# Splitting the keys four tiles ahead, with two more of ten heads copied by ScalarE

## The reference

```
p = h @ w_in[l]
q_a, k_a, v_a, q_b, k_b, v_b = split(p)        # 8 + 2 + 2, then 8 + 8 + 8 heads of 64
q_a = _axial_rope(_rms_norm(q_a, qn_a[l]), row_pos, col_pos)   # likewise k_a; q_b, k_b normed only
o_a = _window_gqa_latent(q_a, k_a, v_a, k_ac, v_ac, sink_a[l])
o_b = _neighbourhood_latent(q_b, k_b, v_b, k_bc, v_bc, rpb_b[l])
```

## Time and profile before

| | |
|---|---|
| three runs | 2680.24, 2682.34 (median), 2683.26 us |
| the profiled execution: its own time | 2682.12 us |
| its span, first to last instruction | 2680.3 us |
| mean granted TensorE clock | 0.960 of full |
| PE busy | 2469.3 us, 92% |
| DVE, ACT, POOL busy | 1621.1, 1061.1, 359.8 us |
| last input panel ends, keys begin | about 362.6 us |
| first scores of the attention | 395.06 us |
| barrier behind the attention | about 757.6 us |

### The profile page before, as it was taken

The page is one execution under the profiler, slowest core; times in us unless marked ns, Lnnn a source line. Parts: engine busy times, 40 slices in busy tenths (PEclk is TensorE's granted clock), DMA queues, the critical chain, the costliest instruction groups (busy, mean ns, idle before and its releaser), DMA issues. The chain is left out here.

```text
span 2680.3 us, 42340 instructions
## 1 busy us (share of the span) xinstructions
PE 2469.3 (92%) x15597; PEld 2129.4 (79%) x15597; DVE 1621.1 (60%) x2701; ACT 1061.1 (40%) x2101; POOL 359.8 (13%) x507
## 2 busy tenths in 40 slices
PE   4799979988969799999999989997897999999998
PEld 2689877777859688888888889995795888878886
DVE  3523237776764977777677942007529777756677
ACT  1422235555641433333344432124435544444443
POOL 2566312221110200000000010003203000000001
PEclk8899989999979899999999999997898999999999
DMA  8233320000032132333275431110131444377463
GB/s 288 94 111 118 117 52 3 1 1 1 1 125 80 71 103 91 118 102 102 99 271 177 154 123 32 48 32 13 47 127 63 157 146 157 130 253 254 133 187 116
DMA packets 189033, 288.15 MB, mean 108 GB/s; under 512 B 11704, under 2 KB 109948, under 8 KB 188540
## 3 DMA queue, kind: packets, MB, share of 16 engines
q1 hardware_dynamic: 188860, 285.84, 31.9%
HBM read 219.46 MB, written 67.34 MB: 107 GB/s over the span
## 5 line engine op out<-in xcount | busy, mean ns | idle before, releaser
L378 PE MATMUL ps<-w_hi,ht_hi 128*128 128x256 f32 x1744 | 504.3, 289 | 18.5 <-DVE w_lo L363 9.8
L379 PE MATMUL ps<-w_lo,ht_hi 128*128 128x256 f32 x1744 | 498.5, 286 | 0.0
L380 PE MATMUL ps<-w_hi,ht_lo 128*128 128x256 f32 x1744 | 498.4, 286 | 0.0
L378 PEld LDWEIGHTS ps<-w_hi,ht_hi 128*128 128x128 f32 x1744 | 338.6, 194 | 35.4 <-DVE w_lo L363 11.7
L379 PEld LDWEIGHTS ps<-w_lo,ht_hi 128*128 128x128 f32 x1744 | 338.6, 194 | 0.0
L380 PEld LDWEIGHTS ps<-w_hi,ht_lo 128*128 128x128 f32 x1744 | 338.2, 194 | 0.0
L363 DVE TENSOR_TENSOR w_lo<-stage,w_hi 128x2048 fp32r<-128x2048 f32 x31 | 73.7, 2377 | 220.9 <-ACT w_hi L359 220.9
L1696 PE MATMUL ps<-ff_b_hi,ff_a_hi 128*128 128x512 f32 x448 | 174.5, 390 | 2.6 <-DVE ff_b_lo L1684 1.4
L1698 PE MATMUL ps<-ff_b_hi,ff_a_lo 128*128 128x512 f32 x448 | 174.3, 389 | 0.0
L1697 PE MATMUL ps<-ff_b_lo,ff_a_hi 128*128 128x512 f32 x448 | 174.3, 389 | 0.0
L1454 PE MATMUL ps<-ht_hi,swiglu_w_hi 128*128 128x512 f32 x352 | 138.2, 393 | 10.1 <-DVE tmp L1964 7.7
(11 more groups left out here) (361 smaller groups left out, 5748.4 us busy)
## 6 DMA issues: line engine op xcount, KB each, us to landing
ff_a_raw<-ff_act_dram SPq DMA_DIRECT2D x112, 256.0 KB, 2.8
stage<-w_in SPq DMA_DIRECT2D x23, 1024.0 KB, 5.2
swiglu_a_raw<-swiglu_act_dram SPq DMA_DIRECT2D x77, 256.0 KB, 3.0
stage<-w_mod SPq DMA_DIRECT2D x16, 1024.0 KB, 5.5
ff_stage<-w_ff SPq DMA_DIRECT2D x16, 1024.0 KB, 5.4
ff_act_dram<-ff_act_sums SPq DMA_DIRECT2D x16, 1024.0 KB, 4.3
ff_act_dram<-ff_acts SPq DMA_DIRECT2D x16, 768.0 KB, 5.7
swiglu_stage<-w_up SPq DMA_DIRECT2D x11, 1024.0 KB, 5.2
```

What stands on the lines that cost most here:

```text
L378: pe.matmul(bank, a, wh[:, k, :], start=(k == 0), stop=False)
L379: pe.matmul(bank, a, wl[:, k, :], start=False, stop=False)
L380: mm = pe.matmul(bank, b, wh[:, k, :], start=False, stop=(k == KT - 1))
```

## The change

`k_split` becomes four buffers of their own, at offsets 0, 5120, 10240 and 24576 of the ring. Those lie on `stage`, on slot 0 of w_hi and on slot 0 of w_lo, which the ninth panel does not use. ScalarE's `hi` of tiles 0 to 3 moves into the ninth panel, behind its copies of rows 4 to 7; `hi` and `lo` of tile j + 4 then follow the copies out of tile j. ScalarE copies heads 8 and 9 too, so that it has six heads of ten, and VectorE four. The loops are written out. The first `hi` waits for the last weight split, the end of the eighth panel, and the normed and rotated keys.

```diff
-    k_split = at("k_split", [2, 10, P], F32, ring)
+    k_split = [at(f"k_split{i}", [10, P], F32, ring + x) for i, x in enumerate((0, 5120, 10240, 24576))]
@@ keys_pe
+            pe.wait_ge(dense_evac, D_O)
+            for j in range(10):
                 pe.wait_ge(ks_lo, j + 1)
-                if late:
+                if j >= 2:
                     pe.wait_ge(kt_a, j - 1)
                     pe.wait_ge(kt_v, j - 1)
                 for h in range(10):
-                    mm = pe.transpose(ps[:, 3 * b + h // 4, (h % 4) * P:(h % 4 + 1) * P], k_split[:, b, h, :], ident[:, :])
+                    mm = pe.transpose(ps[:, 3 * (j % 2) + h // 4, (h % 4) * P:(h % 4 + 1) * P], k_split[j % 4][:, h, :], ident[:, :])
                 mm.then_inc(kt_tr, 1)
+        def key_hi(act, j):
+            if j == 0:
+                act.wait_ge(w_lo_done, P_O)
+                act.wait_ge(*panel_used(P_O - 2))
+                act.wait_ge(hg_done, 10)
+                act.wait_ge(roped, ROPED)
+            if j >= 4:
+                act.wait_ge(kt_tr, j - 3)
+            act.activation(k_split[j % 4][:, :, 0:HD].bitcast(F32R),
+                           row_tile(k_nat, j, 0, KVW).rearrange("p (h d) -> p h d", d=HD), ACT.Copy).then_inc(ks_hi, 1)
@@ keys_act
+            for j in range(10):
                 act.wait_ge(kt_tr, j + 1)
+                act.activation(kt[:, 0:4, j * P:(j + 1) * P], ps[:, 3 * (j % 2), :].rearrange("p (h n) -> p h n", n=P), ACT.Copy)
+                act.activation(kt[:, 8:10, j * P:(j + 1) * P], ps[:, 3 * (j % 2) + 2, 0:2 * P].rearrange("p (h n) -> p h n", n=P),
+                               ACT.Copy).then_inc(kt_a, 1)
+                if j + 4 < 10:
+                    key_hi(act, j + 4)
@@ keys_dve
+            for j in range(4):
+                lo(j)
+            for j in range(10):
+                dve.wait_ge(kt_tr, j + 1)
+                dve.tensor_copy(kt[:, 4:8, j * P:(j + 1) * P], ps[:, 3 * (j % 2) + 1, :].rearrange("p (h n) -> p h n", n=P)).then_inc(kt_v, 1)
+                if j + 4 < 10:
+                    lo(j + 4)
@@ ScalarE's program
+            for n, panel in enumerate(X_PANELS[:8]):
+                heads_act(act, panel, P_X + n + 1, NT, 0, D_X + NT * n, 6 + NT * n)
+            for j in range(NT):
+                act.wait_ge(dense_done, D_X + NT * 8 + j + 1)
+                act.activation(v_nat[:, j, X_PANELS[8][1]:X_PANELS[8][1] + PN], ps[:, j % 4, 0:PN], ACT.Copy).then_inc(dense_evac, 1)
+                if j >= 4:
+                    key_hi(act, j - 4)
             keys_act(act)
```

More of the change, by code:

```diff
@@ L544, in keys_pe @@
         def keys_pe(pe):
-            def tile(j, b, late):
+            pe.wait_ge(dense_evac, D_O)
+            for j in range(10):
                 pe.wait_ge(ks_lo, j + 1)
-                if late:
+                if j >= 2:
                     pe.wait_ge(kt_a, j - 1)
                     pe.wait_ge(kt_v, j - 1)
-                else:
-                    pe.wait_ge(dense_evac, D_O)
                 for h in range(10):
-                    mm = pe.transpose(ps[:, 3 * b + h // 4, (h % 4) * P:(h % 4 + 1) * P], k_split[:, b, h, :], ident[:, :])
+                    mm = pe.transpose(ps[:, 3 * (j % 2) + h // 4, (h % 4) * P:(h % 4 + 1) * P], k_split[j % 4][:, h, :], ident[:, :])
@@ L554, in tile @@
                 mm.then_inc(kt_tr, 1)
[L555 to L559, removed]
-        def keys_act(act):
[L563 to L571, removed]
-                act.wait_ge(kt_tr, j + 1)
[L573 to L586, removed]
@@ L588, in keys_dve, with lo @@
         def keys_dve(dve):
-            def lo(j, b):
+            def lo(j):
                 dve.wait_ge(ks_hi, j + 1)
[L591 to L597, removed]
+                dve.tensor_tensor(k_split[j % 4][:, :, HD:P], row_tile(k_nat, j, 0, KVW).rearrange("p (h d) -> p h d", d=HD),
+                                  k_split[j % 4][:, :, 0:HD], ALU.subtract).then_inc(ks_lo, 1)
@@ L1163, in _ @@
             act_c(act)
-            for n, panel in enumerate(X_PANELS):
-                heads_act(act, panel, P_X + n + 1 if n < 8 else None, NT, 0, D_X + NT * n, 6 + NT * n)
+            for n, panel in enumerate(X_PANELS[:8]):
[5 more added lines that the diff above has]
+                    key_hi(act, j - 4)
             keys_act(act)
```

## The result

The changed kernel took 2660.4 us in the median of five runs (2658.33 to 2666.94), the kernel before 2682.34 us in five beside it (2680.03 to 2684.53). Two more sets of five runs of the same changed kernel (experiments 1 and 12) had medians of 2658.51 and 2664.0 us, with ratios of 0.9922 (0.9908 to 0.9936) and 0.9938 (0.9924 to 0.9951). Over all fifteen the mean is 2662.4 and the median 2663.7 us, from 2656.95 to 2667.08. Over the 52 runs of the kernel before that were made in this study the mean is 2680.5 and the median 2680.3 us, from 2675.17 to 2685.51. So the change is worth some 18 us by the means and 16.6 by the medians.

The account below looks back on a forecast made before the run. The keys were taken as a chain of waits with no engine full. Attention starting 15.5 us earlier, less 0.3 for POOL, gives 15.2 off 2682.12: 2666.9, put at 2667.0 for the median; range 2663.5 to 2674.

Parts of the forecast that it names:

- The start: First key tile: its transposes wait only for the panel's last copy and start at 363.1, not 364.68.
- The steady state: Inside the keys, per tile: TensorE 1.09, ScalarE 1.41, VectorE 1.39 us, none alone the bound; pace 1.55.
- the ring: Keys: waits through ScalarE's copies and `hi`, VectorE's `lo` and copy, and TensorE take 4.64 us for three tiles.
- POOL's contention: POOL's first two query splits fall beside `lo` of tiles 3 and 4 and the first copies: 0.3 us lost.
- The clock: TensorE runs the keys at full speed, busy 75%; a 3.4 us low stretch, if one comes, costs 1 us.
- The loops: Key loops: writing them out costs nothing, as in the dense panel's written-out rows.
- The sum, and behind the keys: Keys save 15.5 - 0.3 = 15.2 us; later stages pass it on, low stretches there up to 1 us each.
- The range: Whole kernel: 2663.5 (sum, 2 us of low stretches, 1.5 of runs' spread) to 2674 (low clock throughout).
- The low clock in the changed keys: Rival, chance 0.14: half speed through the keys, 2.15 us a tile, 8.3 us saved, 2674 us.
- the slower ring: Rival, chance 0.10: five hand-overs in the keys take 0.2 us more each; 9 to 12 saved, 2670 to 2673.
- no change: Rival, chance 0.04: something else holds the attention's start at about 395; time within 0.2% (5.4 us).
- slower: Rival, chance 0.04: low clock reaches into the attention; 82 us of it needed to be slower by 0.2%.

Follow-up runs that it names:

- experiment 12: Changed kernel a third time, with no edit: 2664.0 us, ratio 0.9938.
- experiment 5: Changed kernel with the four first `hi` splits put behind the last panel instead of inside it: 2663.74 us, ratio 0.9947.
- experiment 6: Changed kernel with two buffers, first two tiles split early, the others two tiles ahead, tile by tile: 2665.47 us, ratio 0.9954.
- experiment 7: Changed kernel with three buffers, three tiles split early and the others three tiles ahead: 2662.15 us, ratio 0.9935.
- experiment 9: Kernel before with key loops written out and 10 or 16 unused constant transposes in each TensorE wait of the keys: 2670.01 us, ratio 0.9961.
- experiment 2: Kernel before with only the three key loops written out: 2679.59 us, ratio 0.9998.
- experiment 10: Kernel before with three chained useless ScalarE copies, some 3.2 us, as first work behind the attention's barrier: 2684.82 us, ratio 1.0019.
- 4: Changed kernel with 15 chained useless ScalarE copies, some 17 us, between the last key copy and the attention: 2683.17 us, ratio 1.0009.
- 8: Changed kernel with three short ScalarE copies, some 0.4 us, as first work behind the attention's barrier: 2664.6 us, ratio 0.9945.

## Why the prediction was wrong

**What bounds the kernel, and the mechanism:** right. The keys were a chain of waits by pairs, with nothing full; splitting ahead took the waits away.

**The start:** right. The transposes begin 0.75 us behind the last matmul, for 2.47 before, and the four roundings lie in the panel's gaps. Experiment 5 gives it 2.6 us rather than 1.6, since without it the low clock came back in that trace.

**The steady state:** right, and a little too slow. Forecast 1.55 us a tile by the ring; its one full turn took 1.47 a tile (4.42 us for three). Over all ten tiles it is 1.42, by ScalarE's copies at 363.46 to 376.28, since the first tiles were split early and the last have no split beside them. The ring adds a wait in every third tile (0.95, 0.47). The ring's sums for two and three tiles ahead were confirmed by experiments 6 and 7, 3.75 for 3.97 in the first.

**POOL's contention,** 0.3 us: no more than that. The two `lo` that lay beside POOL's work, at 362.71 and 364.99, took 0.87 and 0.93 us for 0.82.

**The clock:** right for the changed keys, 1.00 throughout in every trace of the changed kernel. What I didn't see is that in the kernel before its cost is itself a matter of chance: 32.9 us in one trace and 34.9 in another of the same key code, so that the saving is 16 or 18 us by the draw. Its part is about 6.4 us by experiment 9 and the earlier trace rows, 8.2 by the other trace.

**The loops** were put at nothing, and that failed: experiment 2 gives them 1.3 us of the saving. The sum doesn't lose by it: it takes the changed kernel's times, walked through without loops, from the measured 395.06, so what the loops cost is in the 15.5.

**The sum, and behind the keys:** here it failed. The term for the keys, 15.2, measured 16.0 in the two profiles. For what lies behind the keys the sum had nothing ("the gain is passed on"), and the range 2 us, at "up to 1 us for each" low stretch. That price, taken from the earlier trace rows, was too small. TensorE alone over the attention's first 60 matmuls, in the kernel before and then in the changed kernel's three traces (the first, experiments 1 and 12), which have one, no, two and one low stretch in them:

```profile
395.06:407.27 12.21, 8.53 (x63) 0.86 0.64 120
378.17:389.12 10.95, 7.14 (x63) 1.00 0.58 108
379.37:393.44 14.07, 10.08 (x63) 0.76 0.43 83
379.61:392.14 12.53, 8.69 (x64) 0.86 0.49 92
```

So a low stretch costs 1.3 to 1.6 us there, and 1.6 in the feed-forward part, where 0.7 come on top (experiment 12). The profiles' other 5.7 us are: 0.9 before the keys, where nothing was changed (362.2 and 361.4 for the panel's last matmul), 1.3 in these first 60 matmuls, 2.3 at the end of the first block's feed-forward part, and 1.2 in pieces that no experiment takes up. Neither the 1.3 nor the 2.3 are the change's: the changed kernel has both slower forms in experiment 12, and the old keys have the faster one of the first in experiments 2 and 9 (10.95 us) and of the second in experiment 10 (107.8).

**The range** is the step that put the result outside. I took 2 us for the low stretches, and 1.5 us for the spread, from three runs that lay within 3 us. The runs of the kernel before spread over 10.3 us once there are 52, those of the changed kernel over 10.1, and its medians of five are 2658.5, 2660.4 and 2664.0. With a spread of 5 us to each side, the low stretches in it, the same sum, 2667, would have had a lower end of 2662 and still missed the first median, by 1.6 us; with the 16 to 18 us that the keys give, it would not. Against all fifteen runs (mean 2662.4, median 2663.7) the forecast is 3 to 5 us too high. There is luck in both directions: the first five runs of the changed kernel came out low, and the pooled median is just inside the range (2663.5), while the 2682.12 that I started from is 1.8 us above the median of the 52 runs. Set against each other as pools, the change saves 16.6 to 18.1 us for the 15.3 forecast.

**The rivals.** The low clock in the changed keys, the slower ring, no change and slower all fell. (The block at 390.94 came behind 2.56 us of idling, not 2.4.) For the changed keys the clock behaved as the cited rule on its resting state has it. The same page of the Trainium skill (TensorE: Matmul & The Clock Gate, "Part 4: PE-mode transpose") also holds that transposes don't count as busy, and that the full clock doesn't engage for them. Here the traces disagree: transposes alone kept 1.00 over 23.1 us in experiment 9, and in experiment 5 it came back during transposes. By that rule the changed keys would have run at half speed, at the 2674 of my rival; I had not weighed it.

**What stays open:** why the delayed kernels (4, 8 and 10) are by their means 2 to 4 us slower than their delays, what the 2 us of experiment 9 outside the keys are, and what decides which low stretches a run gets.

## What to carry to other kernels

When engines hand tiles round, write down the ring that each tile's split goes through, in time, and divide it by the number of tiles ahead: it gives the pace for two, three and four buffers before anything is built, and says when one more buffer buys nothing (of the 16 us here the third gave 3.2 and the fourth 0.5; the other 12.3 came with the new order on two buffers and with the full clock). Price a wait of TensorE twice, once as time and once as the low clock that follows it; filler work can test the second part alone. And take the spread from many runs: three that agree within 3 us had 10 us of spread behind them, and a difference between two traces far behind the change should first be looked for between two traces of one kernel.

## What was not expected of the hardware

- Idle times of 2.2 to 2.6 us ahead of a block of 20 transposes were followed by half clock within the block in 12 of 15 cases (three traces of the old keys), and filling them with constant transposes gave full clock and 10 us.
- Low-clock stretches elsewhere differ between executions of one program, and the same kernel took 2657 to 2667 us.
- A stretch of 3.4 us at half clock cost more than the "up to 1" of the prediction: 1.6 us in the attention's first 60 matmuls, 3.1 for two, and 1.6 at 1529.6 in the feed-forward part. What the stretches cost elsewhere no trace here shows singly.
